# Feed-forward groups 1 and 2: the row factor moved into the inputs' rows, and four weight splits in place of five

## What is computed

```python
def rmsnorm(x, g):
    xf = x.astype(jnp.float32)
    y = xf * lax.rsqrt(jnp.mean(xf * xf, axis=-1, keepdims=True) + NORM_EPS)
    return (y * g.astype(jnp.float32)).astype(x.dtype)

def swiglu(x, w_gate, w_up, w_down):
    return (jax.nn.silu(x @ w_gate) * (x @ w_up)) @ w_down
```

## Time and profile before

| | us |
|---|---|
| median of 3 runs | 1156.87 |
| the profiled execution's own time | 1154.23 |
| its span | 1152.4 |
| TensorE busy | 1079.5 (94%) |
| VectorE busy | 814.0 (71%) |
| ScalarE busy | 447.4 (39%) |
| GpSimd busy | 262.6 (23%) |
| mean granted clock of TensorE | 0.965 of full speed |

### The profile page before, as it was taken

One profiled execution on the slowest core, in us unless ns is written; L12 is line 12 of the kernel. 1 busy time (PEld: TensorE's weight loads), 2 busy tenths in 40 slices (PEclk: granted clock), 3 DMA queues, 4 the chain that ended last, 5 costly groups with the idle time before them and its releaser, 6 DMA issues. The chain is left out here.

```text
span 1152.4 us, 23414 instructions
## 1 busy us (share of the span) xinstructions
PE 1079.5 (94%) x9138; PEld 1050.9 (91%) x9138; DVE 814.0 (71%) x1247; ACT 447.4 (39%) x744; POOL 262.6 (23%) x217
## 2 busy tenths in 40 slices
PE   6999899999999999999798989999999999999996
PEld 6999898999999999999677878999999899999995
DVE  5534899736996787788679447764449994399846
ACT  5333454314544343522144434443235442255520
POOL 0012745123640000120222000000156430345201
PEclk9999999999999899999779899799999999999997
DMA  6321322422233111232601002203122323322312
GB/s 215 108 72 55 110 90 93 129 91 74 73 108 111 55 70 56 70 84 74 67 2 38 2 1 95 74 27 111 62 94 74 109 85 98 110 73 78 123 56 78
DMA packets 35399, 92.04 MB, mean 80 GB/s; under 512 B 10368, under 2 KB 12928, under 8 KB 35328
## 3 DMA queue, kind: packets, MB, share of 16 engines
q1 hardware_dynamic: 34320, 88.78, 24.7%
q10 hardware_dynamic: 1008, 2.27, 0.6%
HBM read 87.76 MB, written 3.28 MB: 79 GB/s over the span
## 5 line engine op out<-in xcount | busy, mean ns | idle before, releaser
L828 PE MATMUL ps<-seven,wh 128*128 128x272 f32 x1024 | 200.6, 292 | 17.6 <-ACT silu L842 17.1
L315 PE MATMUL ps<-xh,wh 128*128 128x272 f32 x816 | 192.4, 298 | 16.7 <-DVE xl L512 8.6
L298 DVE TENSOR_TENSOR wl<-raw,wh 128x1024 fp32r<-128x1024 f32 (+1 forms) x99 | 117.6, 1195 | 102.5 <-ACT wh L293 102.1
L315 PE MATMUL ps<-xh,wl 128*128 128x272 f32 x816 | 188.2, 293 | 0.0
L315 PE MATMUL ps<-xl,wh 128*128 128x272 f32 x816 | 188.1, 293 | 0.0
L828 PEld LDWEIGHTS ps<-seven,wh 128*128 128x128 f32 x1024 | 160.4, 189 | 23.1 <-ACT silu L842 21.8
L293 ACT ACTIVATE wh<-raw 128x1024 fp32r<-128x1024 f32 (+1 forms) x99 | 100.7, 1022 | 165.7 <-PE ps L315 95.4
L315 PE MATMUL ps<-hh,wh 128*128 128x272 f32 x704 | 157.1, 289 | 0.0
L315 PE MATMUL ps<-hh,wl 128*128 128x272 f32 x704 | 155.9, 289 | 0.0
L315 PEld LDWEIGHTS ps<-xh,wh 128*128 128x128 f32 x816 | 138.3, 194 | 19.3 <-DVE wl L298 9.0
L315 PE MATMUL ps<-hl,wh 128*128 128x272 f32 x704 | 155.7, 288 | 0.0
(11 more groups left out here) (347 smaller groups left out, 1849.4 us busy)
## 6 DMA issues: line engine op xcount, KB each, us to landing
raw<-in_w_gu SPq DMA_DIRECT2D x88, 512.0 KB, 4.1
raw<-in_w_d SPq DMA_DIRECT2D x32, 512.0 KB, 3.6
raw<-in_w_in SPq DMA_DIRECT2D x19, 512.0 KB, 3.6
raw<-in_w_d SPq DMA_DIRECT2D x16, 384.0 KB, 3.1
raw<-in_w_out SPq DMA_DIRECT2D x8, 512.0 KB, 3.6
out_y<-x SPq DMA_DIRECT2D x16, 136.0 KB, 1.8
x<-in_x ACTq DMA_DIRECT2D x4, 272.0 KB, 5.6
x<-in_x SPq DMA_DIRECT2D x4, 272.0 KB, 6.7
```

The source lines that it names most:

```text
L298: dve.tensor_tensor(wl[:, s % 4, 0:k, :], raw[:, s % RAW, 0:k, :], wh[:, s % 4, 0:k, :].bitcast(F32), SUB).then_inc(S("w_lo"), 1 + skip)
L315: last = pe.matmul(out[:, n], left[:, s, j], right[:, j, n * H:n * H + H], start=first and opens and j == order[0], stop=final and closes ...
L828: last = pe.matmul(out, left[:, j], right[:, j], start=m in (0, 1, 3) and j == 0 and left is hi and right is high, stop=j == 3 and left is ...
```

## The change

1. VectorE multiplies the rows of x by gain and `rb` at once into `qb` (`rows_mul_dve`). ScalarE and VectorE then write new `xh` and `xl` from `qb` (`rows_hi_act`, `rows_lo_dve`), and the rows of sums follow as before (`sums_hi_act`, `sums_lo_dve`). The multiplication by `rb` in `fast_gate` goes.
2. Group 0's down results are multiplied by `rb` as they leave PSUM. The corrections of epsilon (`var_dve`, the `n_late` products) go, and with them their semaphore steps.
3. The high part of the hidden rows of groups 1 and 2 moves from VectorE to ScalarE (`fast_hidden_hi`), as the last entry of ScalarE's list for a tile, and `hl` becomes the last of VectorE's.
4. The gate's two loaded blocks are products 0 and 1 and are split by one instruction of 1024 columns. There are four splits per tile, and the four sums and the banks are reordered to match.
5. VectorE's and ScalarE's lists for a tile, and the places of the row work in the loops of group 0, are reordered.

```diff
+            if k in (1, 2):
+                act.wait_ge(S("f_sum"), i * 8 + (16 * q + 16 + 4 * n + 2 * k))
             else:
                 landed(act, q, g, i, s)
-            act.wait_ge(S("f_done"), i * 14 + (7 * n + (1, 3, 4, 6, 7)[k]))
+            act.wait_ge(S("f_done"), i * 14 + (7 * n + (2, 4, 6, 7)[k]))
...
             for m, (high, low) in enumerate(rights):
-                pe.wait_ge(S("f_lo"), i * 10 + (10 + 5 * n + (1, 2, 2, 3, 4, 4, 5)[m]))
-                if m == 1:
-                    pe.wait_ge(S("q_lo"), 4 * q + 4)
+                pe.wait_ge(S("f_lo"), i * 8 + (8 + 4 * n + (1, 1, 2, 2, 3, 3, 4)[m]))
+                if m in (0, 2):
+                    pe.wait_ge(S("q_lo"), 8 * q + 7 + m // 2)
                 if m in (2, 4, 5, 6):
-                    pe.wait_ge(S("f_copy"), i * 8 + (4 * n + {2: 1, 4: 3, 5: 2, 6: 4}[m]))
-                out = fast_bank(s, (0, 1, 0, 2, 0, 1, 0)[m])
+                    pe.wait_ge(S("f_copy"), i * 8 + (4 * n + {2: 1, 4: 2, 5: 3, 6: 4}[m]))
+                out = fast_bank(s, (0, 2, 0, 1, 0, 1, 0)[m])
...
-            dve.wait_ge(S("f_part"), i * 6 + (3 * n + 3))
-            dve.tensor_tensor(silu[:, s % 2], silu[:, s % 2], rb[:], MUL).then_inc(S("gate"), 1)
...
+        def fast_hidden_hi(act, q, g, i, s):
+            act.wait_ge(S("h_mul"), i * 2 + (FT * q + GROUPS[g][0] + s + 1 + 2))
+            act.activation(hidden_row(hh, i, s), h32[:, s % 2], ACT.Copy).then_inc(S("h_hi"), 1)
+
+        def fast_hidden_lo(dve, q, g, i, s):
+            dve.wait_ge(S("h_hi"), i * 2 + (FT * q + GROUPS[g][0] + s + 1))
+            dve.tensor_tensor(hidden_row(hl, i, s), h32[:, s % 2], hidden_row(hh, i, s).bitcast(F32), SUB).then_inc(S("h_lo"), 1)
 
         def fast_tile_act(act, q, g, i, s):
             fast_copy(act, q, g, i, s, 0)
             fast_hi(act, q, g, i, s + 1, 0)
             fast_copy(act, q, g, i, s, 1)
             fast_copy(act, q, g, i, s, 2)
             fast_hi(act, q, g, i, s + 1, 1)
+            fast_copy(act, q, g, i, s, 3)
             fast_hi(act, q, g, i, s + 1, 2)
-            fast_copy(act, q, g, i, s, 3)
+            silu_act(act, q, i, GROUPS[g][0], s)
             fast_hi(act, q, g, i, s + 1, 3)
-            silu_act(act, q, i, GROUPS[g][0], s)
-            fast_hi(act, q, g, i, s + 1, 4)
+            fast_hidden_hi(act, q, g, i, s)
 
         def fast_tile_dve(dve, q, g, i, s):
+            fast_first(dve, q, g, i, s)
             fast_lo(dve, q, g, i, s + 1, 0)
             fast_lo(dve, q, g, i, s + 1, 1)
-            fast_first(dve, q, g, i, s)
+            fast_gate(dve, q, g, i, s)
             fast_lo(dve, q, g, i, s + 1, 2)
-            fast_gate(dve, q, g, i, s)
+            fast_hidden(dve, q, g, i, s)
             fast_lo(dve, q, g, i, s + 1, 3)
-            fast_hidden(dve, q, g, i, s)
-            fast_lo(dve, q, g, i, s + 1, 4)
+            fast_hidden_lo(dve, q, g, i, s)
...
+        def rows_mul_dve(dve, q, k):
...
+                dve.wait_ge(S("f_sum"), 80 * q + 4 * k)
+                dve.wait_ge(S("q_lo"), 8 * q + 2 * k - 1)
+            dve.scalar_tensor_tensor(qb[:, 0], x[:, k], par_(f"g{4 * q}", k), rb[:], MUL, MUL)
+            dve.scalar_tensor_tensor(qb[:, 1], x[:, 4 + k], par_(f"g{4 * q}", 4 + k), rb[:], MUL, MUL).then_inc(S("q_row"), 1)
+
+        def rows_hi_act(act, q, k, u):
+
+            act.wait_ge(S("q_row"), 4 * q + k + 1)
+            act.wait_ge(S("unit_done"), SPL + u)
+            act.activation(xh[:, k, 0:H], qb[:, 0, 0:H], ACT.Copy)
+            act.activation(xh[:, 4 + k], qb[:, 1], ACT.Copy).then_inc(S("q_act"), 1)
...
         def rows_lo_dve(dve, q, k):
+            dve.wait_ge(S("q_act"), 8 * q + 2 * k + 1)
+            dve.tensor_tensor(xl[:, k, 0:H], qb[:, 0, 0:H], xh[:, k, 0:H].bitcast(F32), SUB)
+            dve.tensor_tensor(xl[:, 4 + k], qb[:, 1], xh[:, 4 + k].bitcast(F32), SUB).then_inc(S("q_lo"), 1)
...
             if g == 0:
-                dve.tensor_copy(halves(f[:, d]), pair(d % 4)).then_inc(S("d_out"), 1)
+                dve.tensor_tensor(halves(f[:, d]), pair(d % 4), halves(rb[:]), MUL).then_inc(S("d_out"), 1)
...
-                    if s % 2 == 0:
-                        if s:
-                            rows_hi_act(act, q, s // 2 - 1)
-                        rows_act(act, q, s // 2)
-                rows_hi_act(act, q, 3)
+                    if s in (3, 4, 6, 7):
+                        k = (3, 4, 6, 7).index(s)
+                        rows_hi_act(act, q, k, u)
+                        sums_hi_act(act, q, k)
...
                     if s >= 2:
                         down_dve(dve, q, u, g, s - 2, n)
-                    if s > 2 and s % 2:
-                        rows_lo_dve(dve, q, s // 2 - 1)
-                rows_lo_dve(dve, q, 3)
+                    for k in range(4):
+                        if s == (2, 3, 5, 6)[k]:
+                            rows_lo_dve(dve, q, k)
+                        if s == (2, 3, 5, 7)[k]:
+                            sums_lo_dve(dve, q, k)
+                    for k in range(4):
+                        if s == (1, 2, 4, 5)[k]:
+                            rows_mul_dve(dve, q, k)
```

More of the change, by code:

```diff
@@ L737, in sum_ @@
         def sum_(n):
-            return sums[n // 2][:, :, H + P * (n % 2):H + P * (n % 2) + P]
+            at_ = H + P * (n in (0, 3))
+            return sums[n // 2][:, :, at_:at_ + P]
         def both_sums(n):
@@ L744, in left_of @@
         def left_of(s, k):
-            if k in (1, 3):
-                return both_sums(k // 2)
-            return (fast_raw(s, 0)[:, 0:4], None, fast_raw(s, 0)[:, 4:8], None, fast_raw(s, 1)[:, 4:8])[k]
+            if k in (1, 2):
+                return both_sums(k - 1)
+            return fast_raw(s, 1)[:, 4:8] if k else fast_raw(s, 0)
         def left_to(w, k):
-            if k in (1, 3):
-                return two(slots(w, (1, 4)[k // 2], 2))
-            return slots(w, (0, 0, 3, 0, 6)[k])
+            if k in (1, 2):
+                return two(slots(w, 2 * k, 2))
+            return slots(w, 6) if k else slots(w, 0, 2)
         def fast_bank(s, n):
@@ L856, in fast_gate @@
             dve.wait_ge(S("f_done"), i * 14 + (7 * (n + 1) + 6))
-            dve.tensor_tensor(silu[:, s % 2, H:N], fast_bank(s, 1), silu[:, s % 2, H:N], ADD).then_inc(S("f_part"), 1)
-            dve.wait_ge(S("f_part"), i * 6 + (3 * n + 3))
-            dve.tensor_tensor(silu[:, s % 2], silu[:, s % 2], rb[:], MUL).then_inc(S("gate"), 1)
+            dve.tensor_tensor(silu[:, s % 2, H:N], fast_bank(s, 1), silu[:, s % 2, H:N], ADD).then_inc(S("gate"), 1)
         def fast_hidden(dve, q, g, i, s):
@@ L901, in fast_act @@
             f0, nf = GROUPS[g]
-            for k in range(5):
+            for k in range(4):
                 fast_hi(act, q, g, 0, 0, k, u)
@@ L909, in fast_act @@
             fast_copy(act, *end, 0)
-            fast_copy(act, *end, 1)
             for d in range(4):
-                if d in (1, 2):
-                    fast_copy(act, *end, d + 1)
+                if d == 1:
+                    fast_copy(act, *end, 1)
+                    fast_copy(act, *end, 2)
+                if d == 2:
+                    fast_copy(act, *end, 3)
                 if d == 3:
@@ L917, in fast_act @@
                 split_hi(act, u, 0, d, nf)
+            fast_hidden_hi(act, *end)
         def fast_dve(dve, q, g, u, n):
             f0, nf = GROUPS[g]
-            for k, d in enumerate((4, 5, None, 6, 7)):
+            for k, d in enumerate((4, 5, 6, 7)):
                 fast_lo(dve, q, g, 0, 0, k)
-                if d and (g > 1 or d > 5):
+                if g > 1 or d > 5:
                     down_dve(dve, q, u - KD, g - 1, d, n)
@@ L929, in fast_dve @@
             end = (q, g, nf // 2 - 1, 1)
+            fast_first(dve, *end)
             split_lo(dve, u, 0, 0, nf)
-            fast_first(dve, *end)
             split_lo(dve, u, 0, 1, nf)
@@ L935, in fast_dve, with sums_hi_act @@
             fast_hidden(dve, *end)
+            fast_hidden_lo(dve, *end)
             split_lo(dve, u, 0, 3, nf)
-        def rows_act(act, q, k):
+        def rows_mul_dve(dve, q, k):
             if k == 0:
                 if q:
-                    act.wait_ge(S("out"), 6 * 16)
-                act.wait_ge(S("n_rb"), mark(3, 1, 1) + 1 if q else 1)
-                act.wait_ge(S("n_xl"), 3 * KD + 2 * KD if q else KD)
-            else:
-                act.wait_ge(S("f_sum"), 80 * q + 4 * k)
-            act.activation(qb[:, 0], x[:, k], ACT.Copy, scale=par_(f"g{4 * q}", k))
-            act.activation(qb[:, 1], x[:, 4 + k], ACT.Copy, scale=par_(f"g{4 * q}", 4 + k)).then_inc(S("q_act"), 1)
-        def rows_hi_act(act, q, k):
+                    dve.wait_ge(S("out"), 6 * 16)
+                    dve.wait_ge(S("n_rb"), mark(3, 1, 1) + 1)
+                    dve.wait_ge(S("h_x_new"), 4 * KD)
+                else:
+                    dve.wait_ge(S("n_rb"), 1)
+            else:
```

(3 more changed lines are left out.)

69 lines of the change are left out of this document (28 added, 41 removed).

## The result

The changed kernel takes 1176.4 us (median of 4 runs, 1172.09 to 1182.99) against 1156.38 us (4 runs of the kernel before): a ratio of 1.0149, 95% interval 1.0102 to 1.0196. Slower was forecast, at 1165 with a range to 1171, so the sign was right and the time lies outside the range. Run again the ratio was 1.0125 (1.0094 to 1.0156). The execution profiled first was the slowest of its runs, 1182.99 us over a span of 1181.2.

What follows compares the result with a forecast made beforehand. VectorE, busy 88.6 of 92.9 us, was taken to bound the tile stages. Profiled 1154.2 + 8.8 (passages) - 0.5 (tiles) - 0.3 (rest) = 1162.2, on the median 1165 us; range 1140 to 1171, forecast's own 1158 to 1170.

Steps and rivals of the forecast that it cites:

- rival 3: Passages to group 1: slower clock behind longer waits, at most 1.9 us each in two passages, total 1169; chance 0.07.
- The passage: From group 0's down units to group 1: VectorE waits in row rounds delay splits; +4.4 us per block, +8.8 in both.
- Rival 2: Passage: row rounds stay covered, splits in time, +1 us instead of +4.4, total 1158; chance 0.20 shared with a no-effect rival.
- The tile: Tile stages of groups 1 and 2: product 2 stalls 0.85 us per late tile; -0.5 us, bounded by -20.9 and +5.
- the term's own upper bound: Four tile stages of groups 1 and 2: at most +5 us, with a stall of 1.05 us each.
- The 1.0 us taken for the second tile of group 1: Group 1 tile stage: second tile's sums run late, 1.0 us more, making 6.1 us of stalls instead of 5.1.
- Rival 1: Tiles: GpSimd's turns miss the hidden product, stalls vanish; tiles -20.9 us, total 1145; chance 0.31 including mixtures with the forecast.

## Why the prediction was wrong in size

The mechanisms of tile and passage, their places and the sign were right, though little hangs on the sign: the prediction gave slower a chance of 0.38, the same and faster 0.31 each. The sum was half of what was measured in the two blocks, mainly since it held nothing for the clock:

| part, us in two blocks | forecast | measured |
|---|---|---|
| to product 2 of tile 0 | +8.8 | +7.0 |
| group 1 tiles behind it, at full clock | -1.3 | about -0.4 |
| the same, from a lower clock | 0 (rival 3: up to +3.8) | about +5.6 |
| group 2 tiles | +0.8 | +3.3 |
| sum | +8.3 | +15.5 |

The clock's rows, in the columns of the earlier trace rows. First the first block's stretch at the lower clock, after. Then the second block around product 2 of tile 0 with the cast back on VectorE (no late tiles) and with the rounds apart (no waits of the units). Last the earlier copy 0 (no wait of 3.2 us), around product 2 of tile 0 and, in the second block, behind the wait of 2.5 us:

```profile
135.10:141.90 6.80, 6.20 (x27) 6.20 (x28) 4.92 (x6) 2.25 (x6) 6.06 (x3) 0.50 0.42 143
```
```profile
860.00:880.00 20.00, 15.95 (x105) 15.51 (x104) 10.30 (x13) 8.46 (x12) 15.90 (x10) 0.83 0.35 107
```
```profile
865.00:885.00 20.00, 16.20 (x106) 15.77 (x106) 11.66 (x13) 8.28 (x13) 16.69 (x10) 0.83 0.35 106
```
```profile
127.00:145.00 18.00, 16.28 (x126) 15.63 (x125) 11.96 (x13) 8.50 (x12) 14.73 (x9) 1.00 0.36 126
890.00:905.00 15.00, 12.52 (x88) 12.30 (x87) 13.14 (x13) 6.28 (x10) 8.21 (x6) 0.89 0.38 137
```

- **The passage** went as worked out. Units 4 and 6 were idle for 1.85 and 1.36 us, that is 2.0 and 1.5 us late, forecast 1.65 each, and from the first sums to product 2 it was 8.95 us against 8.9. The rounds ran about 0.9 us faster per block than counted, so +4.4 was 3.5. Undoing the queue took it all back. Rival 2, that the rounds stay covered, is out.
- **The tile** stalled as described, by 0.95 us instead of 0.85. The count left out that the second matmul behind a wait starts 0.23 us after the first and not 0.125, and a hand-over of 0.14 us from L852 to the copy (160.38 to 160.52), so a late tile costs 1.06 us. With 24 of them that is +4.8 us on the stalls, which is the term's own upper bound. The 1.0 us taken for the second tile of group 1 did not come.
- **The clock** is the step that failed: the sum put it at nothing and weighed it as an alternative, with a chance of 0.07, though it came together with the forecast's own waits. By the prediction's own sign, a clock below 1.00 in the first block's stage, rival 3 came true beside it. Behind the waits of 1.85, 1.36, 0.87 and 3.22 us the granted clock was 0.97 over the 90.2 us from product 2 of tile 0 on, and 0.96 over the stage. That is 6.8 us at 1.2 GHz in each block, in both profiles. In the 6.2 us of it behind product 2 matmuls start every 0.227 us instead of 0.125, and 27 of them take 2.8 us longer. Rival 3 was priced by the 3.7 us of the earlier trace rows, at 1.9 us for each passage. There the stretch cost nothing: from product 0 to product 2 the kernel before takes 5.3 us in both blocks, with a wait of 0.22 us ahead of product 2 in the second, where the first has 1.27. The Trainium skill, TensorE: Matmul & The Clock Gate, section "Why this matters for your kernels", warns that gaps between matmuls inside a kernel bring the lower clock, and the trace agrees.
- **What brings the lower clock** is shown only in part. Between group 0's down units and the end of group 2, over all profiles and that of the kernel before, the clock fell behind each of the 14 waits of 3.2 us, behind 3 of the 4 waits of 2.2 to 2.5 us, behind 3 of the 12 waits of 1.8 to 2.0 us ahead of unit 4, and behind none of the 0.8 us waits of the tiles. With the 3.2 us wait and those of the units gone together, it is 1.00 there in both blocks of three profiles. How long it stays low behind a wait of 3.2 us is open: 6.8 us in 8 cases, 3.4 us in 6. It was 6.8 without late tiles (the second row above, 0.83 over 20 us) and 6.8 without waits of the units (the third row), so neither of these is needed for it.
- **Rival 1**, that the turns miss the hidden product, is wrong for the change but named the lever: the later start for GpSimd makes it true, at 0.9921. Its 1145 us is 0.990 of the median before, near that.
- **The range** took the upper end of the forecast (1170) and the clock (+3.8) as cases that exclude each other. Together they give 1174, still 2 us short of 1176.4. The part between the blocks, 466.9 us before and 468.5 and 479.2 us in two profiles after, moves by more than that, and the range had nothing for it. By the ratios the changed kernel stands at 1171 to 1174 us on the median before, 14 to 17 us slower where 8 were forecast.

## What to carry to other kernels

Relieving a busy engine is worth nothing if the work lands, on another in-order engine, ahead of something that the bound engine waits for: here VectorE's busy time fell by 16 us in a stage, the stage grew, and putting one ScalarE line behind another made the kernel 2.5% faster. For each moved instruction that waits, ask what is queued behind it and who needs that. And a long wait of TensorE can have a second price, the lower clock behind it. Here it came with every wait of 3.2 us and cost the changed kernel 2.8 us in each block. It is to be added to the sum and not kept as an alternative to it.

## What the runs showed of the hardware

The turns between VectorE and GpSimd on SBUF tensors go in the order of asking, instruction by instruction: after, the sum issued at 157.45 waits for lo 2, which ends at 158.59, and goes ahead of the product issued at 158.50. The two-tensor product takes 428 ns with no sum in its way and 1371 ns on average with one, while a product that reads PSUM takes 0.42 to 0.43 us in both. Counting with this rule gave the events of the tile shown within 0.3 us. The second matmul behind a wait comes 0.23 us after the first, where 0.125 is the pace; at 1.2 GHz the pace is 0.227 us. And the time of one kernel on one chip goes with the granted clock: of six executions of the changed kernel the two at 0.962 and 0.963 took 1170.3 and 1171.5 us, the four at 0.952 to 0.954 took 1176.9 to 1179.5.
